# A streaming-encoder layer on eight cores: which weights get their bf16 copy in the first tile, when the copies are stored, and the planner's numbers

## The reference

```
h = x @ W_in           8 parts of 1024 columns: u | v | q | f | i | og | gA | gB
A = gelu(u) * (W_s LN(gelu(v)) + b)           in blocks of 128 positions
B = HGRN2 recurrence over q, f, i (8 heads), times silu(og)
m = sig(gA) * (A @ W_A) + sig(gB) * (B @ W_B)
x = LN(alpha x + m @ W_o)
ffn = (gelu(dwconv3(x W_gate)) * (x W_val)) @ W_down
e = sig(x W_pg) * (p W_pp)                     the embedding gate
x = LN(alpha x + ffn + e)
```

## Time and profile before

| | us |
|---|---|
| median of 3 runs | 2644.43 |
| the profiled execution | 2651.09 |
| its span, slowest core | 2649.6 |
| spans of the 8 cores | 2616.7 to 2649.6 |
| TensorE matmul busy in it | 2434.6 |

### The profile page before, as it was taken

How to read it: one execution, slowest core, us unless ns; L and a number is a source line. 1 busy time by engine, 2 the same in 40 slices (tenths; PEclk the granted TensorE clock), 3 DMA queues, 4 the chain that set the end, 5 groups by cost and what they waited for, 6 DMA issues and landing times.

```text
span 2649.6 us, 38856 instructions; the slowest of 8 cores (2616.7 to 2649.6 us)
## 1 busy us (share of the span) xinstructions
PE 2434.6 (92%) x13410; PEld 1245.9 (47%) x13666; DVE 1726.0 (65%) x3043; ACT 1582.4 (60%) x2354; POOL 219.1 (8%) x563
## 2 busy tenths in 40 slices
PE   6988899889889989989999999999999999998797
PEld 3544444434445444454455544454444544454343
DVE  4757764748647577564875768756776658655654
ACT  5856774538645478462775657765686648742452
POOL 2111211001210011000010001100010001100010
PEclk9989999999999999999999999999999999999898
DMA  9999687789886757855444554455445454435353
GB/s 183 193 193 183 112 151 127 184 208 186 187 165 178 220 142 195 187 165 180 150 144 135 187 186 131 140 159 165 165 150 152 159 183 142 136 111 172 106 161 120
DMA packets 119710, 430.20 MB, mean 162 GB/s; under 512 B 13280, under 2 KB 13408, under 8 KB 119520
## 3 DMA queue, kind: packets, MB, share of 16 engines
q1 hardware_dynamic: 90576, 326.23, 37.2%
q0 software_dynamic: 28944, 101.46, 24.6%
HBM read 469.84 MB, written 59.24 MB: 200 GB/s over the span
## 4 chain that ended last, share of the span: by engine, by line
PE 75%; DMA 14%; ACT 5%; DVE 3%; issue 2%; POOL 1%; ACTq 0%; POOLq 0%; SPq 0%; DVEq 0%
PE pg L606 65%; DMA sb_wsl<-w_in 4%; PE pg L831 4%; PE pg L645 3%; DMA sb_wsl<-w_up 2%; DMA sb_wsl<-scr_win 2%; DMA sb_xbf<-xT 2%; ACT sb_xbf L901 1%; DMA sb_wsl<-scr_wb 1%; PE pg L956 1%; PE pg L698 1%; DVE sb_resid L760 1%; DVE sb_resid L764 1%; DMA sb_wsl<-scr_wug 1%; PE pg L853 0%
## 5 line engine op out<-in xcount | busy, mean ns | idle before, releaser
L606 PE MATMUL pg<-sb_xbf,sb_wsl 128*128 128x512 bf16 x6232 | 1448.4, 384 | 117.8 <-DMA sb_wsl<-w_in 30.9
L606 PEld LDWEIGHTS pg<-sb_xbf,sb_wsl 128*128 128x128 bf16 x6400 | 620.6, 99 | 841.0 <-issue 163.1
L606 PE MATMUL pg<-sb_arena,sb_wsl 128*128 128x512 bf16 x1376 | 310.5, 379 | 3.7 <-DMA sb_wsl<-w_dn 2.0
L606 PEld LDWEIGHTS pg<-sb_arena,sb_wsl 128*128 128x128 bf16 x1408 | 137.2, 98 | 164.6 <-issue 2.9
L876 DVE SCALAR_TENSOR_TENSOR sb_t32a<-sb_t32a,pg 128x512 f32<-128x512 f32 x96 | 65.9, 686 | 210.2 <-PE pg L606 206.1
L941 DVE TENSOR_TENSOR sb_arena<-pg,sb_t32b 128x512 bf16<-128x512 f32 x176 | 120.6, 688 | 121.2 <-PE pg L606 118.7
L930 DVE SCALAR_TENSOR_TENSOR sb_t32b<-sb_gs,sb_cst,sb_t32b 128x512 f32<-128x512 f32 x176 | 131.4, 748 | 71.4 <-ACT sb_t32b L928 70.8
L870 ACT ACTIVATE sb_t32a<-pg 128x512 f32<-128x512 f32 x96 | 57.2, 597 | 202.0 <-PE pg L606 178.3
L925 POOL COPY sb_cy<-sb_gs 128x2 f32<-128x2 f32 x176 | 50.6, 288 | 1321.1 <-ACT sb_gs L924 1320.9
L924 ACT ACTIVATE sb_gs<-pg 128x512 f32<-128x512 f32 x176 | 104.2, 592 | 91.5 <-PE pg L606 90.5
L710 DVE SCALAR_TENSOR_TENSOR sb_sh<-sb_sh,sb_el,pg 128x128 f32<-128x128 f32 x384 | 131.3, 342 | 37.1 <-PE pg L698 34.4
(11 more groups left out here) (180 smaller groups left out, 3387.9 us busy)
## 6 DMA issues: line engine op xcount, KB each, us to landing
sb_wsl<-scr_win SPq DMA_DIRECT2D x196, 512.0 KB, 4.3
sb_wsl<-scr_wug SPq DMA_DIRECT2D x66, 512.0 KB, 4.1
sb_wsl<-w_in POOLq DMA_DIRECT2D x60, 512.0 KB, 12.7
sb_wsl<-w_up POOLq DMA_DIRECT2D x55, 512.0 KB, 7.2
sb_wsl<-scr_wuv SPq DMA_DIRECT2D x55, 512.0 KB, 3.7
sb_wsl<-scr_wdn SPq DMA_DIRECT2D x40, 512.0 KB, 3.6
scr_win<-sb_wsl SPq DMA_DIRECT2D x32, 512.0 KB, 9.5
sb_resid<-xT SPq DMA_DIRECT2D x32, 512.0 KB, 5.8
```

The source lines that it names most:

```text
L606: last = e.matmul(out, lhsT=slot[:, k * 256 + j * 128:k * 256 + (j + 1) * 128], rhs=rhs3[:, k0 + k, :], start=(k0 + k == 0), stop=(k0 + k ...
```

## The change

Four things. (1) `win0` (u) and `wpg` (embedding gate) get `st` 0: cast in tile 0 and stored there, read from the copy from tile 1 on. (2) The stores of win5, wb, win1 and win0 may be put in SP's queue only after the first matmul that reads the slot has been placed; the store has no real wait on that matmul, only its place moves. (3) The loads of x get a gate that is the same as before for tile 1 and none for later tiles. (4) The keys, rates and latencies that the planner uses move, and each tile has a shift of its own, so the order is worked out anew for all tiles.

```
-H_KEY = (-85.0, -25.0, 15.0, 80.0)
+H_KEY = (-112.695, -25.0, 15.0, 85.167)
...
+LATE_STORE = ("win5", "wb", "win1", "win0")
+CAST_TILES = {"win2": 0, "win3": 0, "win4": 0, "win5": 0, "win0": 0, "win1": 2, "win6": 1, "win7": 2, "wa": 1, "wb":
+              0, "wo": 0, "wug": 1, "wuv": 2, "wpg": 0, "wdn": 2}
...
     def pe(self, ins, outs, fn, cols, n=1):
-        return self._record("pe", ins, outs, fn, n * (cols / 2400.0 + 0.0025))
+        op = self._record("pe", ins, outs, fn, n * (cols / 2400.0 + 0.0025))
+        for b in ins:
+            st = self.held.pop(id(b), None)
+            if st is not None:
+                op.gate.append(st)
+                st.indeg += 1
+        return op
...
-            st = 0 if key[:4] in ("win2", "win3", "win4", "win5") or key[:2] in ("wo", "wb") else (
-                1 if key[:4] in ("win6", "wug0", "wug1") or key[:2] in ("wa", "wu", "wp") and key[:3] != "wuv" else 2)
+            grp = key[:4] if key[:3] == "win" else key[:3] if key[:3] in CAST_TILES else key[:2]
+            st = CAST_TILES[grp]
...
+                    d = fw.dma("sp", lambda v=v: s_wst[nsl[id(v.ap)]], [v], [db],
+                               lambda e, v=v, dr=dr: e.dma_start(out=dr.ap(), in_=v.ap[:, 0:cols]), cols * 128 * 2)
+                    if grp in LATE_STORE:
+                        fw.held[id(v)] = d
...
+                elif t == 1:
+                    after = (gates[X_FIRST[h], 0],)
+                else:
+                    after = (gates[X_AFTER[h], t - 2],) if X_AFTER else ()
...
         for t in range(NT):
-            b0 = (t + 1) * PERIOD
+            b0 = (t + 1) * PERIOD + SHIFT[t]
             if t + 1 < NT:
-                setk(b0 - 110.0, 0.0)
-                load_x(t + 1, (gates["wb0", 0],))
+                setk(b0 + X_KEY, 0.0)
+                load_x(t + 1)
```

More of the change, by code:

```diff
@@ L26 @@
 PERIOD = 300.0
-H_KEY = (-85.0, -25.0, 15.0, 80.0)
+H_KEY = (-112.695, -25.0, 15.0, 85.167)
 H_SPAN = 40.0
-B_KEY, B_SPAN = 0.0, 170.0
-R_KEY, R_SPAN = 172.0, 130.0
-U_KEY, U_EARLY = -18.0, 2
-GBATCH = 4
+B_KEY = -2.024
+B_SPAN = 171.936
+R_KEY = 172.0
+R_SPAN = 130.0
+U_KEY = -15.728
+U_EARLY = 2
+GBATCH = 4
+X_AFTER = ()
+X_FIRST = ("wb0", "wb0")
+X_KEY = -95.647
+X_MUL = 1.412
+ACT_C = 0.215
+DVE_C = 0.19
+LAT = 0.15
+DMA_C = 300.0
+DMA_H = 330.0
+DMA_L1 = 0.944
+DMA_L2 = 1.266
+SLACK_A = 0.6
+SLACK_O = 0.2
+SET_PEN = 12.0
+LATE_STORE = ("win5", "wb", "win1", "win0")
+CAST_TILES = {"win2": 0, "win3": 0, "win4": 0, "win5": 0, "win0": 0, "win1": 2, "win6": 1, "win7": 2, "wa": 1, "wb":
+              0, "wo": 0, "wug": 1, "wuv": 2, "wpg": 0, "wdn": 2}
+FIRST_KEY = 15.0
+FIRST_RATE = 2.0
+PAIR_KEY = 25.0
+MUL_A = 1.0
+MUL_D = 1.0
+SHIFT = (0.0, 3.789, -0.091, 0.0, -0.388, 0.0, -6.384, 0.0, 0.0)
 _CST = {}
@@ L121, in __init__ @@
         self.ends = {}
+        self.held = {}
         self.key = 0.0
@@ L235, in pe @@
     def pe(self, ins, outs, fn, cols, n=1):
-        return self._record("pe", ins, outs, fn, n * (cols / 2400.0 + 0.0025))
+        op = self._record("pe", ins, outs, fn, n * (cols / 2400.0 + 0.0025))
[5 more added lines that the diff above has]
+        return op
     def act(self, ins, outs, fn, n=512, ptrs=0, tset=None):
-        return self._record("act", ins, outs, fn, 0.215 + n / 1200.0 + 0.093 * ptrs, tset)
+        return self._record("act", ins, outs, fn, ACT_C + n / 1200.0 + 0.093 * ptrs, tset)
     def dve(self, ins, outs, fn, n=512, cost=None):
-        return self._record("dve", ins, outs, fn, (cost if cost is not None else 0.16 + n / 960.0) + 0.03)
+        return self._record("dve", ins, outs, fn, (cost if cost is not None else DVE_C - 0.03 + n / 960.0) + 0.03)
     def pool(self, ins, outs, fn, cost):
@@ L286, in schedule @@
         order = []
-        LAT = 0.15
         while left:
@@ L314, in schedule @@
                 for st, op in ready:
-                    if st <= (lo + 0.6 if e == "act" else lo + 0.2):
+                    if st <= (lo + SLACK_A if e == "act" else lo + SLACK_O):
                         k = op.key
                         if op.tset is not None and op.tset != cur:
-                            k += 12.0
+                            k += SET_PEN
                         if pick is None or (k, op.n) < pick[0]:
@@ L326, in schedule @@
             op.st = st
-            cost = op.cost
+            cost = op.cost * (MUL_A if e == "act" else MUL_D if e == "dve" else 1.0)
             if op.tset is not None and op.tset != cur:
@@ L337, in schedule @@
             if op.dsem is not None:
-                b = max(dma_free, st + 1.0)
-                dma_free = b + op.nbytes / (300000.0 if q_cast(op) else 330000.0)
-                end = dma_free + 1.2
+                b = max(dma_free, st + DMA_L1)
+                dma_free = b + op.nbytes / (1000.0 * (DMA_C if q_cast(op) else DMA_H))
+                end = dma_free + DMA_L2
             else:
@@ L526, in wload @@
             if first:
[L527 to L528 removed]
+                pool = W0 if key[:4] in ("win0", "win1", "win2", "win3", "win4", "win5") else W1
             v = VT(pool)
             chain = (prev_load[id(pool)],) if id(pool) in prev_load and not first else ()
[L531 to L532 removed]
+            grp = key[:4] if key[:3] == "win" else key[:3] if key[:3] in CAST_TILES else key[:2]
+            st = CAST_TILES[grp]
             chain = chain + tuple(after)
@@ L544, in wload @@
                     scratch[key] = (dr, db)
-                    fw.dma("sp", lambda v=v: s_wst[nsl[id(v.ap)]], [v], [db],
-                           lambda e, v=v, dr=dr: e.dma_start(out=dr.ap(), in_=v.ap[:, 0:cols]), cols * 128 * 2)
+                    d = fw.dma("sp", lambda v=v: s_wst[nsl[id(v.ap)]], [v], [db],
+                               lambda e, v=v, dr=dr: e.dma_start(out=dr.ap(), in_=v.ap[:, 0:cols]), cols * 128 * 2)
+                    if grp in LATE_STORE:
+                        fw.held[id(v)] = d
             else:
@@ L560, in build, with load_x @@
         fw.key = -100.0
-        def load_x(t, after=()):
+        def load_x(t):
             q = t % 2
[L564 to L567, removed]
+            n = 2 if t == 0 else len(X_AFTER) or 2
+            w = KC // n
+            for h in range(n):
+                if t == 0:
+                    after = ()
+                elif t == 1:
+                    after = (gates[X_FIRST[h], 0],)
+                else:
+                    after = (gates[X_AFTER[h], t - 2],) if X_AFTER else ()
+                fw.dma("pool", s_x[q], [], XBs[q][w * h:w * h + w], lambda e, h=h, q=q, t=t: e.dma_start(
+                    out=xbfs[q][:, w * h:w * h + w, :],
+                    in_=xT[t, :, h * w * TT:(h + 1) * w * TT].rearrange("p (k t) -> p k t", t=TT)), X_MUL * w * TT * 512, after)
         fw.dma("sp", s_cst, [], [CST], lambda e: e.dma_start(out=cst[:], in_=cst_d), 128 * NCST * 4)
@@ L996, in build @@
         for p in range(4):
-            h_stage(0, 25.0 * p - H_KEY[p], (p,))
-        setk(15.0, 2.0)
+            h_stage(0, PAIR_KEY * p - H_KEY[p], (p,))
+        setk(FIRST_KEY, FIRST_RATE)
         sgu_setup()
```

## The result

The changed kernel takes 2620.07 us, the median of 5 runs (2616.36 to 3041.54), the kernel before beside it 2642.90 us (2641.49 to 2649.99). The ratio is 0.9903, 95% interval [0.9879, 0.9927]: 25.6 us faster, between 19 and 32. Runs in which one die of the chip was granted a far lower clock are left out of this ratio, and of all that follow.

The account below looks back on a forecast made before the run. The prediction took the kernel as bound by PE, its matmuls filling 92% of the span; its terms summed to -7.9 us, taking the median 2644.43 to 2636.5, rounded 2636 us, range 2612 to 2658.

Parts of the forecast that it names:

- rival C: Tiles 1 and 2 (500 to 1100): DMA relief and new order free half the excess idle time; -26 us, 2618; chance 0.15.
- Embedding gate, tile 1: Tile 1: the 4.92 us wait for a cast load shrinks as it becomes a copy load; -3.5 us, bounds -4.9 and 0.
- u, tiles 1 and 2: 500 to 800 and 800 to 1100: less DMA share cuts PE's excess idle time proportionally; -4.4 and -2.0 us.
- Tile 0: Tile 0: added u stores on full DMA cost +2 us, bounds -2 and +6.4; gate stores in its b_stage +0.5.
- Late stores: Slots with late stores: freed only when the store lands, delaying the next loads; +1.5 us, bounds 0 and +20.
- The order anew: PE's swapped order: 0 in later tiles, bounds +8 and -8; -2 us in tiles 0 to 2, bounds +6 and -8.
- the 1.5 that was named as a sign of being wrong: Later tiles: the forecast would be wrong if their period moved by more than 1.5 us.
- The 8.02 us wait for wb: Tile 1: PE waits 8.02 us for wb3, its slot held by the store of win6_3; this wait stays.

Follow-up runs that it names:

- f_c: Kernel before with its TensorE, ScalarE and VectorE order held, but u and embedding gate cast in tile 0 only; ratio 0.9997, middle core -3.1 us.
- f_o: Kernel before's casts, stores and rates, with the three engines held to the order of n_only; ratio 0.9934, middle core -18.8 us.
- f_a: Changed kernel's engine order held, with the kernel before's casts and stores, DMA queues planned with new rates and latencies; ratio 0.9943, middle core -12.9 us.
- cn: Changed kernel without the late stores; two runs, 2619.20 and 2626.39 us, no ratio; middle core -21.8 us against the kernel before.
- n_only: Kernel before with only the planner's new numbers and the new gate of x, casts and stores unchanged; ratio 0.9958, middle core -16.4 us.
- f_w60: Changed kernel with its engine order held, but win6 cast in tile 0 alone; 2610.80 us, ratio 0.9868 to the kernel before.
- l_only: Kernel before with only the late stores of win5, wb, win1 and win0 added; ratio 1.0004, middle core +0.1 us.
- f_w62: Changed kernel with its engine order held, but win6 cast in tiles 0 to 2 and stored in tile 2; ratio 0.9938 to the kernel before.
- c_only: Kernel before with only the new casts of u and embedding gate, old numbers, no late stores; ratio 1.0009, middle core -2.5 us.
- cl: Kernel before with the new casts and the late stores together, old planner numbers; ratio 0.9995, middle core -6.4 us.

## Why the prediction was right, and where it was not

It said faster as the likeliest, 2636 us in 2612 to 2658; 2620.07 is inside. The size was off by a factor of three (-7.9 against -25.6 us), and the near hit of rival C's 2618 is not its mechanism: C wanted DMA relief to free the early tiles and the new order to use the room; the relief alone is f_c's 3.1 us, and f_o gains 18.8 us with no room made.

*Embedding gate, tile 1* (-3.5): right for the wait, a little small. The wait for w_pg, 5.0 us at the mean of the cores, is 0.1 us for the copy. Either part alone does much of that: the new casts alone leave 1.9 us (f_c), the new order alone 2.3 us (f_o). And in f_c the next wait grew, that for x in 600 to 800 from 2.0 to 4.1 us, so a wait saved is not yet time saved.

*u, tiles 1 and 2* (-4.4 and -2.0): over-sized when taken alone. With the gate's part and tile 0 the forecast has -7.4 us for what f_c measured as -3.1. To read excess idle time off the DMA share as if one made the other was the mistake: in f_c the share of 500 to 800 fell by 0.063, as forecast (0.066), and the longest wait stayed. But the relief is not worth the same under every order: f_a against the changed kernel makes it 10 to 17 us (with the late stores in it), cn against n_only 5.4 us (two runs, another chip).

*Tile 0* (+2, +0.5): f_c's first norm of tile 0 comes 0.3 us later in its profile, the changed kernel's 5.1 us later; with the order changed too, this can't be parted. Four further stores cost 4 us (f_w60). The size was fair.

*Late stores* (+1.5): 0.1 us at the middle core (l_only).

*The order anew* (0 in the later tiles, -2 in tiles 0 to 2): this is the step that failed. With the casts of before the order of n_only is worth -18.8 us (f_o), that of the changed kernel -12.9 us (f_a), in place of -2. Between the first norm of tile 3 and that of tile 7 (the second VectorE instruction of each norm, median core) the changed kernel gains 5.6 us and f_o 8.1 us, at the bound of 8 and not 0; that is 1.4 and 2.0 us a period, the latter more than the 1.5 that was named as a sign of being wrong. The rest of f_o's gain, about 11 us, lies almost all ahead of that, beyond the bound of -8 that stood for tiles 0 to 2. The forecast judged the swaps by the neighbours of the loads, and took it that small swaps leave waits as they are. What they do is put work between two waits of PE, and in the example above that counts twice: the wait is covered, and the clock falls for a shorter time. Every wait row of the trace was read for its own length only, and the clock column, there in the earlier trace rows, was not read.

*The 8.02 us wait for wb*: the forecast had the wait rightly staying, for the wrong reason. The store in the slot puts the load off by 5 to 7 us against its use, and without it the backlog costs nearly the same (f_w62).

## What to carry to other kernels

When a change lets a planner order the work anew, measure the order by itself: hold the engines' order fixed and change the transfers, then the other way round. A saving in DMA is worth what the order makes of it, here about 3 us under the old order and, by two rough comparisons, 5 to 17 under the new. For an engine bound by short waits, sum its time at the low clock beside its waits, over all runs and not one profile, and look for waits that lie close together.

## What the runs showed of the hardware

In some runs two neighbouring cores are granted 0.81 of the full clock for a long stretch of tile 0, a level that lies between the two seen elsewhere. Core 2 of c_only:

```profile
100.00:150.00 50.00, 41.82 (x288) 22.94 (x288) 39.20 (x80) 38.53 (x60) 6.34 (x12) 0.96 1.03 214
150.00:200.00 50.00, 46.96 (x197) 21.23 (x197) 14.84 (x22) 19.60 (x27) 4.22 (x8) 0.79 0.98 192
200.00:250.00 50.00, 50.00 (x214) 22.19 (x212) 30.40 (x51) 16.36 (x25) 3.69 (x7) 0.81 0.83 175
```

It ended at 2652.7 us where the middle core of that execution ended at 2615. A mean clock of 0.970 or less, which such a stretch leaves, was seen on 9 of 48 core spans of c_only, 14 of 72 of cl, 4 of 40 of n_only, and on none of 152 of the kernel before on the same chip, 48 of l_only or 48 of f_c (another chip). A run with such a core ends late: c_only's four took 2643.82 to 2656.84 us, its two without 2632.95 and 2634.75. This is why its slowest core gained nothing where its middle core gained 2.5 us. What sets it off stays open; PE was busy for 94% of 150 to 200, with a DMA share of 0.98, when it began. Core 2 showed 0.8125 from 160.9 to 322.4 us of its record, save 3.4 us; at full use that is 0.19 x 158 = 30 us.
